# Thirty-two modulation rows loaded into buffers of their own, and a neighbourhood attention with token-major values and a joined mask and maximum

## The reference, cut to what matters

```python
def first_block(x, c, ...):
    mod = c_act @ w_ada[l] + b_ada[l]
    sh_a, sc_a, gt_a, sh_f, sc_f, gt_f = [m[:, None, :] for m in jnp.split(mod, 6, axis=-1)]
    ...
    h = _rmsnorm(x, norm_ffn[l]) * (1.0 + sc_f) + sh_f
    gate, up = jnp.split(h @ w_gate_up[l], 2, axis=-1)
    x = x + gt_f * ((jax.nn.silu(gate) * up) @ w_down[l])
```

```python
def second_block(x, w_in, ...):
    h = rms_norm(x, pre_mix_g[l])
    proj = h @ w_in[l]
    a, gate, q, k, v = jnp.split(proj, splits, axis=-1)
    yc = conformer_conv_group(a, gate, ...)       # 31 taps over tokens, then a layer norm and silu
    ya = neighbourhood_attention_group(q, k, v, rpb[l])
    mix = jnp.concatenate([yc, ya], axis=-1) @ w_out[l]

def neighbourhood_attention_group(q, k, v, rpb):
    ...
    s = jnp.where(col_mask[:, None, :], s + bias, NEG_INF)
    p = jax.nn.softmax(s.reshape(...), axis=-1)
    o = jnp.einsum("bhrwkv,brkvhd->brwhd", p, v_rows)
```

## Time and profile before

| what | us |
|---|---|
| median of 3 runs | 2725.5 |
| the profiled execution, whole | 2724.88 |
| its span, first to last instruction | 2722.8 |
| PE busy | 2670.6 |
| DVE busy | 1915.2 |
| ACT busy | 1290.7 |
| POOL busy | 140.1 |

### The profile page before, as it was taken

One profiled execution on the slowest core, in us unless ns is written; L12 is line 12 of the kernel. 1 busy time (PEld: TensorE's weight loads), 2 busy tenths in 40 slices (PEclk: granted clock), 3 DMA queues, 4 the chain that ended last, 5 costly groups with the idle time before them and its releaser, 6 DMA issues.

```text
span 2722.8 us, 39658 instructions
## 1 busy us (share of the span) xinstructions
PE 2670.6 (98%) x15550; PEld 2340.8 (86%) x15550; DVE 1915.2 (70%) x2919; ACT 1290.7 (47%) x1981; POOL 140.1 (5%) x126
## 2 busy tenths in 40 slices
PE   8999999999999999999999999999999999999998
PEld 7788988888898878888888889998888888888887
DVE  6887776877887886565555679996667465575665
ACT  2165643434435444444444554567564444443443
POOL 0000000000011000000000270111200000000000
PEclk9999999999999999999999999999999999999999
DMA  9954366767786786555555555553545555555554
GB/s 387 409 191 155 104 208 209 255 222 235 269 290 229 273 285 220 186 192 188 188 191 187 188 183 173 182 169 128 186 153 192 193 189 193 191 188 193 191 190 146
DMA packets 158731, 565.10 MB, mean 208 GB/s; under 512 B 17616, under 2 KB 21840, under 8 KB 158416
## 3 DMA queue, kind: packets, MB, share of 16 engines
q1 hardware_dynamic: 158544, 562.56, 60.2%
HBM read 560.39 MB, written 2.10 MB: 207 GB/s over the span
## 4 chain that ended last, share of the span: by engine, by line
PE 83%; DVE 9%; DMA 4%; issue 2%; ACT 2%; DVEq 0%; ACTq 0%; SPq 0%
PE BK L369 15%; PE BK L367 15%; PE BK L371 8%; PE BK L366 7%; PE BK L383 7%; PE BK L384 7%; PE BK L387 7%; DVE LO L751 3%; PE BK L376 3%; PE BK L373 3%; PE BK L374 3%; PE BK L398 2%; DMA RAW<-wst_dram 2%; DVE B L993 2%; PE BK L487 1%
## 5 line engine op out<-in xcount | busy, mean ns | idle before, releaser
L587 ACT ACTIVATE HI<-RAW 128x1024 fp32r<-128x1024 f32 x824 | 873.3, 1060 | 1184.5 <-PE BK L367 490.1
L751 DVE TENSOR_TENSOR LO<-RAW,HI 128x1024 fp32r<-128x1024 f32 x824 | 1010.6, 1227 | 360.5 <-ACT HI L587 359.5
L369 PE MATMUL BK<-H,HI 128*128 128x512 f32 x1896 | 750.8, 399 | 0.6 <-DVE H L787 0.4
L367 PE MATMUL BK<-H,HI 128*128 128x512 f32 x1864 | 733.5, 396 | 0.0
L371 PE MATMUL BK<-H,LO 128*128 128x256 f32 x1896 | 528.3, 279 | 13.0 <-DVE LO L751 12.9
L366 PE MATMUL BK<-H,LO 128*128 128x256 f32 x1864 | 520.3, 279 | 0.2 <-DVE H L789 0.2
L371 PEld LDWEIGHTS BK<-H,LO 128*128 128x128 f32 x1896 | 356.5, 188 | 96.1 <-DVE LO L751 20.9
L366 PEld LDWEIGHTS BK<-H,LO 128*128 128x128 f32 x1864 | 350.0, 188 | 80.6 <-DVE H L789 0.6
L369 PEld LDWEIGHTS BK<-H,HI 128*128 128x128 f32 x1896 | 359.7, 190 | 8.0 <-issue 1.7
L383 PE MATMUL BK<-HI,H 128*128 128x512 f32 x896 | 361.4, 403 | 1.0 <-DVE H L789 0.6
L367 PEld LDWEIGHTS BK<-H,HI 128*128 128x128 f32 x1864 | 349.5, 188 | 3.7
(11 more groups left out here) (281 smaller groups left out, 2447.4 us busy)
## 6 DMA issues: line engine op xcount, KB each, us to landing
RAW<-wst_dram SPq DMA_DIRECT2D x837, 512.0 KB, 3.3
RAW<-wada_dram SPq DMA_DIRECT2D x155, 512.0 KB, 4.9
EARLY<-wada_dram SPq DMA_DIRECT2D x37, 512.0 KB, 10.7
EARLY<-wst_dram SPq DMA_DIRECT2D x19, 512.0 KB, 12.1
X<-xT_dram SPq DMA_DIRECT2D x8, 512.0 KB, 7.2
B<-bias_dram SPq DMA_DIRECT2D x32, 128.0 KB, 3.3
out_dram<-B SPq DMA_DIRECT2D x8, 256.0 KB, 2.2
B<-gain_dram SPq DMA_DIRECT2D x1, 1024.0 KB, 4.8
```

Of the source, the lines that this page charges most:

```text
L367: e.matmul(bk[:, :], hh, H[:, k, :], start=False, stop=last, skip_group_check=True).then_inc(S["tile"], 1)
L369: e.matmul(bk[:, :], hh, H[:, k, :], start=first, stop=False, skip_group_check=True)
L587: e.activation(HI[:, u % NHL, :], raw_at(slot), ACT.Copy).then_inc(S["hi"], 1)
L751: e.tensor_tensor(LO[:, u % NHL, :], raw_at(slot), HI[:, u % NHL, :].bitcast(f32), sub).then_inc(S["lo"], 1)
```

## The change

It has two parts. First, the last 32 modulation units are a kind of their own, "B". They go to four buffers `FAR`, which lie in `B1` and are free from `mid` on, while the weights keep the ring of five to themselves; and they are spread over units 239 to 289, five to every eight weight units. The memsets of `B1` and `B2` (`blanks`) wait for the last of them. Second, in the second block: the values are made by `tile_tokens` straight in token order, ahead of the queries and keys, and ACT writes them with one instruction for four head pairs (`value_rows`); mask and maximum are one DVE instruction, `tensor_tensor_reduce` (also in the first block's attention); the column mask is in the bias table that is loaded, and ACT scales this table by the inverse of the factor (`bias_scaled`, two items ahead), so that POOL has no part; and the taps are handed out by `PACE` (quarters of a pair of taps per unit: six, then four, eight, ten) instead of four taps per unit.

```diff
-NRAW, NEARLY, NHL = 5, 8, 3
+NRAW, NEARLY, NHL, NLATE = 5, 8, 3, 4
+FAR_AT, FAR_RATE = 236, 10
+PACE = (6, 4, 8, 10, 5)
...
+        FAR = B1[:, 0:16, :].rearrange("p (i a) t -> p i (a t)", i=NLATE)
+        NV = [t.rearrange("p a t -> p (a t)").rearrange("p (j m n) -> p j m n", j=4, m=2) for t in (B1[:, 17:23, :], B2[:, 0:6, :])]
...
+            def bias_scaled(i, loaded, factor):
+                q.wait_ge(loaded, factor)
+                e.activation(BB[i % 4], BB[i % 4], ACT.Copy, scale=RI[:, i % 2:i % 2 + 1]).then_inc(S["at_a"], 1)
...
-            def turned_rows(dst, src, scale, done, free):
+            def value_rows(g, m, src, done, free):
                 q.wait_ge(done, free)
-                for m in range(2):
-                    r = e.activation(dst[:, m, :].rearrange("p (s n) -> p s n", s=3)[:, 0:3:2, :], m2h(src[:, 128 * m:128 * m + 128]), ACT.Copy, scale=scale[:, m:m + 1])
-                r.then_inc(S["at_a"], 1)
+                dst = NV[g][:, :, m, :].rearrange("p j (s n) -> p j s n", s=3)[:, :, 0:3:2, :]
+                e.activation(dst, src.rearrange("p (j h n) -> p j h n", j=4, h=2), ACT.Copy, scale=RV[:, m:m + 1]).then_inc(S["at_a"], 1)
...
-            def na_mask(p, ps, i, scores, bias, free):
+            def na_mask(p, ps, i, c, scores, bias, free):
                 q.wait_ge(scores, bias, free)
-                e.scalar_tensor_tensor(p, ps, RQ[:, i % 2:i % 2 + 1], BB[i % 4], mult, add).then_inc(S["at_v"], 1)
+                e.tensor_tensor_reduce(p, ps, BB[i % 4], RQ[:, i % 2:i % 2 + 1], 3e38, add, ALU.min, SM[:, c:c + 1]).then_inc(S["at_v"], 1)
...
-            def soft_max(p, c, masked):
-                q.wait_ge(masked)
-                e.tensor_reduce(SM[:, c:c + 1], p, AX, ALU.max, negate=True).then_inc(S["at_v"], 1)
...
-            def bias_mask(i, loaded):
-                q.wait_ge(loaded)
-                e.tensor_tensor(BB[i % 4], BB[i % 4], cn("nm"), add).then_inc(S["at_g"], 1)
...
-                due = min(N_ADA, put if i < 80 else 64 + (i - 80) * 3 // 4 if i < 176 else 136 if i < 192 else min(160, 136 + (i - 192) * 7 // 8) if i < 236 else 160 + (i - 236) * 3 // 4)
-                kinds += ["L"] + ["A"] * max(0, due - put)
-                put = max(put, due)
+                due = min(160, put if i < 80 else 64 + (i - 80) * 3 // 4 if i < 176 else 136 if i < 192 else 136 + (i - 192) * 7 // 8)
+                far = 0 if i < FAR_AT else min(32, (i - FAR_AT) * FAR_RATE // 16)
+                kinds += ["L"] + ["A"] * max(0, due - put) + ["B"] * (far - n_far)
+                put, n_far = max(put, due), far
...
             def blanks():
-                blank["pad"] = do("pad_zero", "cv_v", mid, n=2)
+                while st["na"] < N_ADA:
+                    yield
+                far_end = [mid, ("ada", w.count["ada"])]
+                blank["pad"] = do("pad_zero", "cv_v", far_end, n=2)
...
-            CONV_STEP = 2
+            CONV_STEP = 1
...
-            def e_v(key):
-                HD[key] = None
-
+            nv_tok = {}
+
+            def e_v(g, m):
                 def f(bk, tok, own):
-                    i, t, fr = tv.get()
-                    k = copy_out(t, bk, tok, own, fr)
-                    yield
-                    mi, mk, mf = mbank.get()
-                    m = do("turn", "at_p", mk, t, 2, k, mf)
-                    tv.release(i, m)
-                    yield
-                    vi, vt, vf = vt_r.get()
-                    a = do("turned_rows", "at_a", vt, mk, RV, [m, need(r_tok, "rq")], vf)
-                    mbank.release(mi, a)
-                    HD[key] = (vi, vt, a)
+                    nv_tok[g, m] = do("value_rows", "at_a", g, m, bk[:, :], [tok, need(r_tok, "rq")], blank["value", g])
+                    own[0].release(own[1], nv_tok[g, m])
+                    yield
                 return f
...
+            for g in range(2):
+                for _ in token_blocks(H1, u_tok2, 0, "w_in2", 0, 32 + 4 * g, lambda m: e_v(g, m)):
+                    convolve(PACE[1])
...
             for j in range(1, 8):
-                gen = make2(j)
-                for _ in range(6):
-                    next(gen, None)
-                    next(cg, None)
+                for _ in make2(j):
                     if step < 4 * j:
                         pipe_step(stages, step, 32)
                         step += 1
-                run(gen)
+                    convolve(PACE[3])
...
-            later(drain())
+            later(drain(), 0, PACE[4])
```

More of the change, by code:

```diff
@@ L57, in const_array @@
     put("mm", np.where(k <= 128 + s, 0.0, -1e30))
-    start = np.clip(s % 64 - 8, 0, 48)
-    put("nm", np.where((k % 64 >= start) & (k % 64 < start + 16), 0.0, -1e30))
     rot = np.zeros((128, 128), np.float32)
@@ L2100, in walk @@
             mid = now()
+            far_free[0] = mid
             spin(4)
@@ L2311, in walk, with scale_bias @@
             xg = xs_gen()
+            due = [0]
             for j in range(8):
-                for _ in block(H1, u_tok2, 0, "w_in2", 0, j, e_a(j)):
-                    next(cg, None)
-                for _ in block(H1, u_tok2, 0, "w_in2", 0, 8 + j, e_g(j)):
-                    next(cg, None)
+                for n, ev in ((j, e_a(j)), (8 + j, e_g(j))):
+                    for _ in block(H1, u_tok2, 0, "w_in2", 0, n, ev):
+                        due[0] += PACE[0]
+                        while due[0] >= 4:
+                            due[0] -= 4
+                            next(cg, None)
             b_used = [b2_free] * 4
-            bm_tok = {}
+            bl_tok, bm_tok = {}, {}
             def next_bias(i):
-                d = load("load_bias", f"bias{i % 4}", i, b_used[i % 4])
-                bm_tok[i] = do("bias_mask", "at_g", i, d)
+                bl_tok[i] = load("load_bias", f"bias{i % 4}", i, b_used[i % 4])
+            def scale_bias(i):
+                bm_tok[i] = do("bias_scaled", "at_a", i, bl_tok[i], need(r_tok, "rq"))
             def e_r(ring, key):
@@ L2659 @@
     dc = np.clip(c[None, :] - c[:, None], -15, 15) + 15
-    bias = I["rpb_2"][0][:, dr[:, None, :, None], dc[None, :, None, :]].reshape(32, 128, 256)
+    left = np.clip(c - 8, 0, 48)[:, None]
+    dc = np.where((c[None, :] >= left) & (c[None, :] < left + 16), dc, 31)
+    table = np.full((16, 15, 32), -1e30, np.float32)
+    table[:, :, 0:31] = I["rpb_2"][0]
+    bias = table[:, dr[:, None, :, None], dc[None, :, None, :]].reshape(32, 128, 256)
     arrays = {
```

107 lines of the change are left out of this document (63 added, 44 removed).

## The result

| | before | after |
|---|---|---|
| median (runs) | 2725.02 us (4) | 2710.76 us (4) |
| lowest to highest | 2724.47 to 2725.96 | 2709.18 to 2712.7 |
| the profiled execution, whole | 2724.88 | 2710.69 |
| its span | 2722.8 | 2708.9 |
| PE, DVE, ACT, POOL busy | 2670.6, 1915.2, 1290.7, 140.1 | 2664.3, 1893.6, 1299.7, 108.1 |

A forecast was written before the change was run, and what follows sets the result against it. PE was taken as the bound, busy for 2670.6 of 2722.8 us. The terms -8.2 - 4.5 - 2.7 + 0 + 0 = -15.4 us, put on the median of 2725.5, gave 2710 us; range 2701 to 2719.

The forecast's parts named there:

- part 1: First feed-forward part, modulation units: all nine PE waits for `LO` go, -8.2 us, ends 0 and -9.5.
- part 2b: First stretch of the projection: three taps per unit instead of four end PE's losses, -2.7 us, ends 0 and -3.5.
- below 80%: Sign to look for in the first feed-forward part: DVE's busy share falls below 80%.
- Part 2a: Values made token-major: cheaper units -2.7 us, no turns on PE -1.8 us, together -4.5 us, bound -4 to -5.
- Part 2c: Units with a softmax step: DVE at 3.83 us stays just behind PE's 3.96, booked 0, upper end +2.6 us.
- The DVE rival: Attention's step units: taps keep 0.49 us, DVE needs 4.29 us per unit, 7.3 us given back, 2717 us; chance 0.11.
- The bias-load rival: Step units: `bias_scaled` waits for its load and holds ACT, 30 items lose 1.2 us each, 2746 us; chance 0.05.
- Part 2d: End of the projection, where the convolution's norm meets the remaining softmax steps: booked 0, ends -4 and +6 us.
- The rival of a crowded end: End of the projection: ACT's overrun is exposed and bank waits remain, +6 us, 2716 us; chance 0.12.
- The waits that I thought wider steps would relieve: From 1840 to 1920 us: steps every six tiles instead of four should relieve the waits making up 5.1 us.
- The page rule on the table load: End of the projection: 1283 ns plus about 1380 ns drain per switch, two adding 2.8 us to ACT, term +3.

The follow-up runs named there:

- e1 to e3: Kernel before plus, in turn: new buffers and spacing of the modulation units, 2715.3 us; the spacing alone, 2714.65 us; the buffers alone, 2714.56 us.
- e7: The kernel after with the first three bias loads issued ahead of the value blocks, eight units earlier: 2709.7 us.
- e5: The kernel after with four taps per unit again in the first stretch of the projection (eight quarters instead of six): 2713.8 us.
- e10: e7 with four output rows instead of five in the first group of `w_out2`, holding one PSUM bank less: 2705.75 us.
- e9: The kernel after with only the values back to the old feature-major way, turned by PE and written by ACT: 2713.93 us.
- e4: The kernel after with the modulation units back in the shared ring at their old spacing: 2717.93 us.

## Why the prediction was right, and where it wasn't

The time was right (2710 against 2710.76) and so was the main mechanism. Three terms were off, and by luck their errors partly cancelled: 3.0 us too little for part 1, 1.9 us too much for part 2b, 3.8 us too little loss at the end. What they leave is a gain of 12.5 us behind unit 224 where I had booked 15.4. That the medians differ by 14.3 all the same is luck too: 1.4 us of it stand ahead of unit 224 in the profiled executions, in the stretch that moves by itself.

*Part 1: forecast -8.2, measured -11.2 by the marks and -9.6 to -10.3 by the medians of e1 to e3.* The chain (late load, ACT, `LO`, PE) was right. The size was read from idle time alone. Summed from start to start, PE's ten slow places in that stretch are 10.0 us and not 8.2, since a modelled end of a matmul reaches into the wait behind it. The matmul behind each of the ten starts another 0.1 us late, which makes 11.1. My upper end of -9.5 was too near. That the buffers and the spacing each suffice, I had not seen; and DVE fell by nothing (118.23 us of 140, 84%, where I wrote below 80%), because PE's higher pace asks for more `LO`.

*Part 2a: forecast -4.5.* 16 units at 2.72 us (43.5 us from unit 520 to 536) against 2.87 are -2.4, the turns -1.8: -4.2, inside the bound.

*Part 2b: forecast -2.7. This step failed.* I took the 2.7 us of idle time from 1684 to 1740 for waits for `LO`, because DVE was at 56.00 of 56. The waits of the kernel before from 1700 to 1740 us say otherwise:

```profile
PE BK L520 <- ACT B L673: 1.6, 1, 1.6
...
PE BK L376 <- DVE LO L751: 0.9, 1, 0.9
```

1.6 us were the first softmax step. PE's turn of it (L520) waits for ACT's scale, and that for DVE's share, which stands behind a unit's four taps. DVE, ACT and PE of the kernel before:

```profile
1736.58 2.04 DVE L993 SCALAR_TENSOR_TENSOR B<-B,CO 128x256 f32<-128x256 f32 x4
1738.54 0.15 DVE L934 RECIPROCAL SC<-SC 128x1 f32<-128x1 f32 x1
```

```profile
1738.73 0.51 ACT L673 ACTIVATE B<-B,SC 128x256 f32<-128x256 f32 x1 [1.20 <-DVE SC L934]
```

```profile
1739.29 0.44 PE L520 MATMUL BK<-CN,B 128*128 128x128 f32 x2 [1.56 <-ACT B L673]
```

So the full DVE had a hand in this wait as well, but not by `LO`, and three taps a unit ahead of the values don't touch it. The kernel after has a wait of 1.7 us at its own first step, at 1750.9, and e7 shows that the late bias loads made that one. What the slower taps could save was 0.9 us, 1.35 from start to start; e5 gave 0.7 back. With the new `LO` wait of 0.6 us at 1744.7 the term comes to some -0.8. In e7, which has neither wait, the stretch to 568 is 7.4 us shorter (-8.5 without the moved step), where parts 2a and 2b were to give 7.2.

*Part 2c: forecast 0, held.* The period of a unit with a step is 3.97 us and PE's idle in 80 us of them 0.11. The joined mask has 475 ns of busy time and 0.40 us from start to start, against my 0.46. DVE ends at 76.68 of 80 us, 96%: close. The DVE rival did not come. The bias-load rival came once, at a price of 2.3 us (e7) and not 36: ACT's 3.8 us at 1741, at the one place where SP issued three of them at once behind three weight loads; between 1763 and 1925 us ACT waits for no bias load.

*Part 2d: forecast 0, measured +3.8.* The rival of a crowded end came true, at less than its price of +6, and one half of its mechanism was wrong: the bank waits that it named carry the larger part (e10), an overrun of ACT did not show (44.11 of 60 us busy), and the clock comes on top (below). The waits that I thought wider steps would relieve got worse; that the norm among them did it is argued, since e9 moves both. The page rule on the table load ("ScalarE: Activation LUTs", section "What ACT_TABLE_LOAD costs", in the Trainium skill) would have added a drain; the loads of e7 at 1863.32 and 1872.91 take 1.28 us, and the next instruction starts 0.01 us behind. No drain is seen.

To unit 568 the named parts make -2.4 - 1.8 - 0.8 (`LO`: -1.35 + 0.56) + 0.1 (first step) = -4.9, where -5.1 was measured. From there to unit 600 PE idles 5.75 us against 3.1, +2.7, and the matmuls at the lower clock take some 1.6 us longer: +4.3, where +3.8 was measured. What e4 gained in the shared ring stays open.

## What to carry over

A ring that is late shows as long waits of an engine two steps ahead of the bound, and it need only be slowed or widened until those waits no longer reach the bound (2.4 us here, against 3.8); test each half by itself before building both. Read an idle sum by its releasers before giving it to one wait of a full engine beside it, and ask of each releaser what it stood behind itself: here 1.6 of 2.7 us went another way than by `LO`. Look too at how many loads an engine comes to at once: three small ones behind three large ones cost 2.3 us (e7). Where work is moved into a dense stretch, count PSUM banks as well as engine time: a wait "for" an instruction whose data isn't needed can be one for the bank that it gives back (L820), or the view may name what merely ended last (L626); the order of the queues tells which.
